# Two transformer blocks in one kernel: weight splits spread over the mixers' loops, masks placed elsewhere, one modulation group moved

## The reference

```python
logits = einsum(q, k) * scale + (c[t] - c[s])      # c = cumsum(log_sigmoid(ff + b_forget))
logits = where(s <= t, logits, -1e30); p = softmax(logits)
merged = sigmoid(gate_r) * y_ret + sigmoid(gate_f) * y_fox;  out = merged @ w_out
```

## Time and profile before

| what | value |
|---|---|
| median of 3 runs | 2633.13 us (2628.21 to 2635.54) |
| the profiled execution | 2638.64 us, of which the span 2636.5 us |
| granted TensorE clock, mean | 0.946 |
| busy: PE, PEld, DVE, ACT | 89%, 72%, 62%, 50% |
| HBM over the span | 225 GB/s |

### The profile page before, as it was taken

One profiled execution on the slowest core, in us unless ns is written; L12 is line 12 of the kernel. 1 busy time (PEld: TensorE's weight loads), 2 busy tenths in 40 slices (PEclk: granted clock), 3 DMA queues, 4 the chain that ended last, 5 costly groups with the idle time before them and its releaser, 6 DMA issues. The chain is left out here.

```text
span 2636.5 us, 29077 instructions
## 1 busy us (share of the span) xinstructions
PE 2357.1 (89%) x11416; PEld 1886.3 (72%) x11416; DVE 1629.8 (62%) x2345; ACT 1330.7 (50%) x2010; POOL 155.4 (6%) x146
## 2 busy tenths in 40 slices
PE   8998979999999979999899986999957985999983
PEld 6887657888888757788776665878746754788851
DVE  5556245655555625555643568898877477788852
ACT  5555434555555534455423431777852351787740
POOL 0001000000000100000000000011112100011101
PEclk9999889999999978999999997999988987999997
DMA  7765465576676553576622554999983304899983
GB/s 254 254 235 169 151 231 174 181 251 239 209 248 229 162 186 102 186 255 234 210 80 99 184 188 157 344 337 365 367 311 96 113 1 140 300 364 351 347 315 116
DMA packets 177694, 575.75 MB, mean 218 GB/s; under 512 B 20101, under 2 KB 28741, under 8 KB 145808
## 3 DMA queue, kind: packets, MB, share of 16 engines
q1 hardware_dynamic: 153120, 503.96, 54.7%
q10 hardware_dynamic: 13776, 51.58, 4.9%
q0 software_dynamic: 10656, 18.29, 2.0%
HBM read 538.63 MB, written 55.67 MB: 225 GB/s over the span
## 5 line engine op out<-in xcount | busy, mean ns | idle before, releaser
L319 DVE TENSOR_TENSOR LO<-RAW,HI 128x1024 fp32r<-128x1024 f32 x558 | 660.8, 1223 | 216.8 <-ACT HI L305 214.7
L305 ACT ACTIVATE HI<-RAW 128x1024 fp32r<-128x1024 f32 x558 | 570.1, 1055 | 354.4 <-PE PS L377 196.4
L375 PE MATMUL PS<-HI,FR 128*128 128x512 f32 (+2 forms) x1808 | 698.7, 386 | 26.0 <-DVE FR L443 6.6
L377 PE MATMUL PS<-HI,FR 128*128 128x512 f32 (+2 forms) x1808 | 691.7, 383 | 0.0
L376 PE MATMUL PS<-LO,FR 128*128 128x512 f32 (+2 forms) x1808 | 691.0, 382 | 0.0
L305 ACT ACTIVATE HI<-RAW,SM 128x512 fp32r<-128x512 f32 (+2 forms) x576 | 360.5, 681 | 309.5 <-PE PS L377 159.2
L321 DVE SCALAR_TENSOR_TENSOR LO<-RAW,SM,HI 128x512 fp32r<-128x512 f32 (+2 forms) x576 | 378.8, 710 | 211.3 <-ACT HI L305 211.1
L375 PEld LDWEIGHTS PS<-HI,FR 128*128 128x128 f32 x1808 | 344.9, 191 | 97.3 <-issue 11.0
L377 PEld LDWEIGHTS PS<-HI,FR 128*128 128x128 f32 x1808 | 344.8, 191 | 66.2
L376 PEld LDWEIGHTS PS<-LO,FR 128*128 128x128 f32 x1808 | 345.1, 191 | 63.1
L439 ACT ACTIVATE FR<-PS 128x512 fp32r<-128x512 f32 x224 | 122.2, 587 | 234.2 <-PE PS L420 228.3
(11 more groups left out here) (312 smaller groups left out, 2349.0 us busy)
## 6 DMA issues: line engine op xcount, KB each, us to landing
RAW<-in_w_ffn_in SPq DMA_DIRECT2D x88, 1024.0 KB
RAW<-in_w_gate SPq DMA_DIRECT2D x68, 1024.0 KB, 6.0
RAW<-in_w_up SPq DMA_DIRECT2D x68, 1024.0 KB, 6.5
RAW<-in_w_down SPq DMA_DIRECT2D x64, 1024.0 KB
RAW<-in_w_ada SPq DMA_DIRECT2D x48, 1024.0 KB
RAW<-in_w_ffn_out SPq DMA_DIRECT2D x44, 1024.0 KB
RAW<-in_w_in SPq DMA_DIRECT2D x44, 1024.0 KB
YD<-CN ACTq DMA_DIRECT2D x32, 1024.0 KB, 4.9
```

The costliest lines, as they stand in the source:

```text
L305: e.activation(HI[:, i % NSPLIT, c], raw_of(j)[:, c], ACT.Copy, scale=1.0 if g is None else g).then_inc(*hi_done.up())
L319: e.tensor_tensor(LO[:, i % NSPLIT, c], raw_of(j)[:, c], hi, ALU.subtract).then_inc(*lo_done.up())
L375: e.matmul(o, h, hi[:, j, :], start=first and k + j == 0, stop=False)
L377: x = e.matmul(o, ll, hi[:, j, :], start=False, stop=end)
```

## The change

In the mixers' loops, the fill no longer splits; from turn 6 (first mixer) or 4 (second), each turn splits one part of what follows. The causal mask goes into the broadcast log gates (`below`, an own tile `lfM` in `GB` for the first 128 keys), and two products become one of 256 columns. The band's masks and the identity are copied to rounded tiles once. Group (1,1) leaves the window attention, whose fill is now advanced every second turn, and goes into the routing of the first expert layer, with bank 5 kept out of the rotation until it is done.

```diff
@@ constants
+    t["below"] = np.where(i[:, None] == i[None, :] + 1, 1e30, 0.0)
+        MK = sb("MK", [P, 384], F32R)
@@ hi_parts (lo_parts in the same way, with until_low)
-        def hi_parts(e, q, m):
-            while split_hi[0] < until(m):
+        def hi_parts(e, q, m, most=NSPLIT):
+            for _ in range(min(most, until(m) - split_hi[0])):
@@ act_cond
+            for i, n in enumerate(("ident", "cmask", "wmask")):
+                e.activation(MK[:, P * i:P * i + P], C[n], ACT.Copy).then_inc(*act.up("masks" if i == 2 else None))
-        side = {(0, 0): 0, (0, 1): 1, (0, 2): 0, (1, 0): 0, (1, 1): 1, (1, 2): 0}
+        side = {(0, 0): 0, (0, 1): 1, (0, 2): 0, (1, 0): 0, (1, 1): 0, (1, 2): 1}
@@ act_ada (dve_ada in the same way, with lo_parts)
-                    for m in of[f"ada {l}{g}{k}"]:
-                        hi_parts(e, q, m)
+                    if s not in SPLIT_FROM:
+                        hi_parts(e, q, of[f"ada {l}{g}{k}"][0])
+        SPLIT_FROM = {"mix0": 6, "mix1": 4}
+        lfM = GB[:, 0, :].rearrange("p (h c) -> p h c", h=8)
+        tri_ones = CN[:, 129:385]
@@ pe_mix
-                        e.matmul(B[:, 0:P], lfB[:, 0, h, :], C["negtri"], start=False, stop=False)
                         if t == 0:
-                            x = e.matmul(B[:, 0:P], ident, C["cmask"], start=False, stop=True)
+                            x = e.matmul(B[:, 0:P], lfM[:, h, :], C["negtri"], start=False, stop=True)
                         else:
-                            e.matmul(B[:, P:256], lfB[:, 0, h, :], C["negones"], start=False, stop=False)
-                            e.matmul(B[:, P:256], lfB[:, 1, h, :], C["negtri"], start=False, stop=False)
-                            x = e.matmul(B[:, P:256], ident, C["cmask"], start=False, stop=True)
+                            e.matmul(B[:, 0:256], lfB[:, 0, h, :], tri_ones, start=False, stop=False)
+                            x = e.matmul(B[:, P:256], lfB[:, 1, h, :], C["negtri"], start=False, stop=True)
@@ act_mix, in the loop behind next(fill) (dve_mix in the same way, with lo_parts)
+                if i >= SPLIT_FROM[s]:
+                    hi_parts(e, q, of["ada %d%d7" % M_FILL[l][-1]][0], 1)
@@ dve_mix
-                e.tensor_copy(lfB[:, t, :, :], z.unsqueeze(2).to_broadcast([P, 8, P])).then_inc(
-                    *dve.up(f"{s} lfB {t}"))
+                if t == 0:
+                    e.tensor_copy(lfB[:, 0, :, :], z.unsqueeze(2).to_broadcast([P, 8, P])).then_inc(*dve.up())
+                e.tensor_tensor((lfM, lfB[:, 1, :, :])[t], z.unsqueeze(2).to_broadcast([P, 8, P]),
+                                C["below"].unsqueeze(1).to_broadcast([P, 8, P]), ALU.add).then_inc(*dve.up(f"{s} lfB {t}"))
@@ window attention
-        A_FILL = [(1, 0), (1, 1), (1, 2)]
+        A_FILL = [(1, 0), (1, 2)]
-                            m, mask = (PS[b][:, P:256], C["cmask"]) if t == 0 else (PS[b][:, 0:P], C["wmask"])
-                            e.matmul(m, ident, mask, start=False, stop=True).then_inc(*pe.up(f"{s} qk {u}"))
+                            m, mask = (PS[b][:, P:256], MK[:, P:256]) if t == 0 else (PS[b][:, 0:P], MK[:, 256:384])
+                            e.matmul(m, MK[:, 0:P], mask, start=False, stop=True).then_inc(*pe.up(f"{s} qk {u}"))
-                if i % 4 < 3:
+                if i % 2 == 0:
                     next(fill, None)
@@ pe_attn_out
-            s, tiles, rot = f"o{l}", O_TILES[l], Banks(list(range(8)))
+            s, tiles, rot = f"o{l}", O_TILES[l], Banks([0, 1, 2, 3, 4, 6, 7])
@@ pe_moe: X_FILL = [[(1, 1)], []], result in x_fold_t[:, 0:512]
+            fill = pe_ada(e, q, s, X_FILL[l])
             if NT > 2:
                 logits(0, 2).then_inc(*pe.up())
+            more_fill(1)
             pe_hidden_T(e, q, s, (NT - 1,), HBS, rot)
+            more_fill(1)
             logits(NT - 2, NT).then_inc(*pe.up(f"{s} logits"))
...
+            more_fill(3)
             q.wait_ge(*dve.at(f"{s} chosen"))
...
+            more_fill(2)
             pe_places(e, q, l, rot)
+            for _ in fill:
+                pass
+            rot = Banks(list(range(8)))
             gather_T(0)
@@ act_moe
+            fill = act_ada(e, q, s, X_FILL[l], x_stage, lambda v: [])
+            next(fill, None)
             for m in of[f"{s} router"]:
                 hi_parts(e, q, m)
...
+            for _ in range(7):
+                next(fill, None)
             gather_hi(0)
             for i in range(NE + 1):
+                if i == 1:
+                    for _ in fill:
+                        pass
@@ dve_moe
             dve_list(e, q, l)
+            for _ in dve_ada(e, q, s, X_FILL[l], x_stage):
+                pass
             gather_lo(0)
             for i in range(NE + 1):
+                if l == 0 and i == 4:
+                    q.wait_ge(*mod_out[0].at("mod 11"))
@@ sp_moe, behind the gains
+            sp_ada(e, q, s, X_FILL[l])
```

More of the change, by code:

```diff
@@ L26 @@
           ("cos1", 128), ("sin1", 128), ("cos2", 128), ("sin2", 128), ("iota", 128), ("tid", 4), ("lt4", 16),
-          ("eoff", 16), ("row", 16)]
+          ("eoff", 16), ("row", 16), ("below", 128)]
 def constants():
@@ L307, in hi_parts, with lo_parts @@
                 hi_done.also(j)
-        def lo_parts(e, q, m):
-            while split_lo[0] < until_low(m):
+        def lo_parts(e, q, m, most=NSPLIT):
+            for _ in range(min(most, until_low(m) - split_lo[0])):
                 i = split_lo[0]
@@ L778, in dve_ada @@
                 for k in range(8):
-                    for m in of[f"ada {l}{g}{k}"]:
-                        lo_parts(e, q, m)
+                    if s not in SPLIT_FROM:
+                        lo_parts(e, q, of[f"ada {l}{g}{k}"][0])
                     yield
@@ L1183, in dve_mix @@
                     next(fill, None)
+                if i >= SPLIT_FROM[s]:
+                    lo_parts(e, q, of["ada %d%d7" % M_FILL[l][-1]][0], 1)
                 if i < 8:
@@ L1525, in pe_attn_a @@
             rot3 = Banks([0, 1, 2, 3, 4])
+            q.wait_ge(*act.at("masks"))
             q.wait_ge(*dve.at(f"{s} q scaled"))
@@ L1765, in act_attn_out @@
             q.wait_ge(*dve.at(("qa half 31", "qb normed 1")[l]))
-            for g in (1, 2):
+            for g in ((0, 2), (1, 2))[l]:
                 q.wait_ge(*mod_out[side[1, g]].at(f"mod 1{g}"))
@@ L2109, in pe_down @@
                     pe.also(f"used {m}")
+        X_FILL = [[(1, 1)], []]
+        x_stage = [x_fold_t[:, 0:512], None]
         def pe_moe(e, q, l, rot):
@@ L2126, in logits, with more_fill @@
                 return x
+            fill = pe_ada(e, q, s, X_FILL[l])
+            def more_fill(n):
+                for _ in range(n):
+                    next(fill, None)
             pe_hidden_T(e, q, s, (NT - 2,), HBS, rot)
```

## The result

The changed kernel takes 2600.79 us (median of 4 runs, 2598.35 to 2606.20), the kernel before 2634.34 (4 runs): ratio 0.9882, 95% interval 0.9861 to 0.9902, so 26 to 37 us less. The forecast was 2603, in a range of 2589 to 2622. The profiled execution after took 2598.35 us, the one before 2638.64: their spans differ by 40.2 us, some 7 more than the medians. Where those 7 us lie is one of the questions of the experiments.

What follows compares the result with a forecast made beforehand. TensorE, busy for 89% of the span, was taken as the bound. Terms 13.5 + 9.5 - 0.5 + 12 - 3 = 31.5 us, taken as 30 off the median 2633.13, gave 2603 us, range 2589 to 2622.

Steps and rivals of the forecast that it cites:

- First mixer: First mixer's loop: splitting a part a turn removes the stall at turn 4, net 13.5 us saved, bounds 9 and 16.
- At full clock: First mixer's loop: with the stall gone, turn 7's about 3.5 us at full clock was the price for turns 5 and 6.
- The lighter masks: Both mixers: one fp32 product less per unit in the decay products, 1 us saved in the first, 2 in the second.
- Second mixer: Second mixer's loop: without the split in turn 0, 12.5 us back, 3 lost to later splits, net 9.5, bounds 4 and 13.
- VectorE's addition: Ahead of each mixer's first decay: one tile more and an addition for a copy, 1.8 us lost a mixer.
- Banded masks: First half of the attention loop: 32 rounded masks at 0.11 us each save 3.5 us, bounds 0 and 7.
- Modulation out of the attention loop: Attention loop: eight parts fewer save 4.6 us (first half), 2 (second), and 2 from fewer stores and separated splits.
- Routing: First expert layer's routing: taking eight modulation parts costs net 3 us, bounds 0 and 12 lost.
- VectorE pays: Routing: four low parts of expert 0 and an addition delay VectorE before the first gathered rows, 3.7 us lost.
- The slower rival: Routing: expert 0's weights come too late, the choice chain slips, 30 us exposed, 2636 us; chance 0.06.
- Split in series: Mixers' loops: each part holds both engines ahead of the exps, nine turns pay 2.7 us, 2612 to 2622; chance 0.17.
- The signs of being wrong: Turns from 6 on over 5 us, ScalarE waiting for the gate's transfer, or expert 0's first matmul waiting for a landing.

Runs made afterwards that it cites:

- b0: The kernel before, unchanged, run once more for its stages; 2634.68 us, ratio 1.0016.
- a0: The changed kernel, run once more to compare executions stage by stage; 2599.94 us, ratio 0.9888.
- e5: Changed kernel with the causal mask outside the decay products again, as copies and a product of its own; 2602.02 us, ratio 0.9893.
- e2: Changed kernel with the mixers' splits back in the modulation's fill, the other parts kept; 2618.75 us, ratio 0.9952.
- e4: Changed kernel with the banded masks plain fp32 again instead of rounded copies; 2616.51 us, ratio 0.9940, its profiled execution 2606.77.
- e3: Changed kernel with modulation (1,1) back in the attention loop; 2608.09 us, ratio 0.9906.
- e7: Changed kernel with all five splits in one turn (turn 6 first loop, turn 4 second), not one a turn; 2607.31 us, ratio 0.9906.
- e6: Changed kernel with expert 0's four low parts done behind the gathered rows instead of in the routing; 2602.95 us, ratio 0.9896.
- g1: Changed kernel with expert 0's up weights held back until the first gather has landed; 2606.54 us, ratio 0.9905.
- x2: Changed kernel with one modulation part more ahead of the last hidden tile in the routing; 2597.93 us, ratio 0.9870.
- e1: Kernel before with only the mixers' spread splits added; 2615.35 us, ratio 0.9926.
- x1: Changed kernel with splits one a turn in the attention loop's second half too; 2603.85 us, ratio 0.9905.

## Why the prediction was right, and where its steps failed

The time from the start to expert 0's first matmul is the part that the terms describe: 1644.46 and 1642.36 us in the two executions before, 1612.55 and 1614.29 after. That is 28 to 32 us less, for a sum of 31.5. The stages that the terms name give 30.6 of it (before against after) or 25.2 (b0 against a0); the other 1.4 and 2.9 us lie in stretches between them that the change doesn't touch.

- **First mixer, 12.7 forecast (13.5 for the split, 1 for the masks, 1.8 against), 9.4 to 10.8 measured.** The stall is gone and the gate's first matmul comes 12.5 to 13.3 us sooner after turn 0, as said. Two sizes were off. "At full clock" was wrong in places: turn 6 ran at 0.66, and the gate's product began cold and took 1.6 us more, which no term had. And from turn 7 to the gate the parts cost 1.7 us (8.43 against 6.73), where I had 1.2. The lighter masks, 1 forecast, are worth 1.4 to 1.7 by e5.
- **Second mixer, 9.7 forecast, 4.8 to 7.8 measured.** Turns 0 to 4 gave 13.8 (12.5 forecast), turn 4 to the gate took 3.2 back (3 forecast): the loop is right. The steps that failed are again the clock at the gate's start, 1.4 us, and the lighter masks, of which I had 2 in all turns and e5 shows 0.4 to 0.8; in the unspread loop of e2 they are worth 2.4 to 3.5, because there the turns stand on TensorE (turns 4 to 6 take 0.5 us less each, the products that are gone).
- **VectorE's addition** cost 1.1 to 1.7 us a mixer, forecast 1.8. The row of two full tensors was a good price for two broadcasts.
- **Banded masks**, 3.5 forecast, 4.0 by e4's profile: nearer to the row (0.11 a mask) than to the estimate of 5.3 that the Trainium skill's weight rule (TensorE: Matmul & The Clock Gate, Weight-path perf modes) would give. The rule isn't seen here: the weight load's median is 189 ns for the rounded masks, 192 for the plain ones. e4's timed runs leave room for doubt.
- **Modulation out of the attention loop**, 4.6 + 2 + 2 forecast, 4.6 + 3.8 measured (e3). Right in mechanism; the first half right to the tenth is luck, since that half was 72.7 or 72.8 us in six kernels and 73.4 in two more (e5, e7) with the same loop. The loop as a whole became 12.7 to 13.8 us shorter, forecast 12.
- **Routing**, -3 forecast, -1.7 to -1.8 measured from output product to expert 0. The size was about right and the reason wrong. "VectorE pays" fell with e6: its parts are covered. What pays is the gather, 4.2 us late beside the weights that used to have landed (e3, g1). Against it stand 2.3 us from a clock that was not forecast as such: the output product starts warm (1 us) and the logits are formed warm (1.3, 4.93 to 3.59 us from first logit to scores), where I had 0.7.
- **The slower rival** had its sign all but met, and not its price. I said that it decides when the DMA share from 1609 to 1641 comes to 1.00; the stretch that corresponds shows 0.98, its last 21 us 1.01. But the fifth part had landed: it is multiplied from 1582.71 without a wait, ahead of the choice at 1588.72. Nothing in the choice slipped (6.35 us from scores to ranks, as before), and of 30 us only the gather's 4.2 came. By the trace's landing times eight of the twelve chunks landed between 1577 and expert 0, the first four before; the last one was there at 1611.94, ahead of expert 0's first matmul at 1612.55. The sign was that of full transfers, and these cost only what somebody waits for: here one gather, not twelve chunks. The Trainium skill (DMA: Bandwidth & Descriptors, Queues, rings and completion order) has the engines go round the queues that have work; with g1's weights out of the way the same gather takes 4.5 us instead of 8.7, which agrees; the order of packets in an engine is in no trace here.
- **Split in series** is out by the loops' length; e7 shows that even a burst in one turn costs 2 to 4 us a loop, 1 to 2 with the warm gate behind it.
- **The signs of being wrong.** One was met by a hair: turn 6 of the first mixer took 5.04 us, over the 5 that I had named, and the reason is the clock (0.66 over it; 4.33 us at 1.00 in x2, whose loop is the same). The longest wait for an exp in the two loops was 2.03 us, under the 2.5. "The clock behind turn 4 should be 1.00" failed. From choice to expert 0's first matmul it took 4.2 us more where I had 3. The first matmul of expert 0 did not wait for a landing itself, but the transposes ahead of it did, for 8.08 us.

The sum came out because a shortfall in the mixers (4 us before against after, 8 by b0 against a0) met a surplus of 1 or 2 each in the attention loop and the routing, and because the change of the medians (33.6) holds 2 to 5 us more than the stages up to expert 0. These lie behind it, in a part that I had taken to stay as it was. Right to 2 us was partly luck; right within the range was not.

## What to carry to other kernels

A helper that prepares the next stage's weights is placed by when they land, and only then by how many fit a turn: moving it behind the landing gave most of the gain (some 15 of 18 us by the stages), spreading it the rest, and in the shorter turns of the attention loop spreading gave nothing. When loads are moved toward a stage with a small dependent gather, count what is in flight when the gather is issued, not only whether TensorE has room. And compare two executions of one kernel stage by stage before a difference in a long stage that streams its weights is put down to a change, and add up what lies outside the stages that were forecast.

## What the runs showed of the hardware that I had not expected

The granted clock does not follow from the waits alone. Kernels with the same wait ahead of turn 6 differ: behind 1.52 us of idle time turn 6 ran at 0.66 in the changed kernel; in e7, behind 1.52 as well, and in e1, behind 1.54, it ran at 1.00. The two short waits ahead of the gate (0.87 and 0.85 us) left its start cold in the changed kernel, in e1, e3, e4, e5, e6 and g1 (28.7 to 29.0 us for the product) and in x2 (29.8), also where turn 6 had run warm (e1, e5, x2). Behind the same two waits x1 began it warm (27.3). In e7 it was warm too, but there TensorE had no wait just ahead of it.

At the end of the attention loop x2 had nearly the waits of the changed kernel (3.61 and 2.19 us against 3.71 and 1.78) and more time at half speed. Its second half took 62.4 us instead of 60.1, and from the output product, which began cold, to the scores it took 65.6 instead of 63.2:

```profile
1521.50:1528.00 6.50, 6.50 (x20) 5.16 (x20) 1.82 (x2) 0.00 (x0) 0.00 (x0) 0.62 0.61 209
```

So 1 to 2.5 us can come into a stage or leave it that the edit has not touched. What sets it isn't shown by these runs; a difference of that size in one stage is no verdict on an edit.
